# Moving vector-engine work of a two-block transformer kernel from steps with weight sums to steps with whole tiles

## The reference

```python
# block 1
proj = rmsnorm(x, norm_attn) @ w_in            # q, k, v of kinds A and B
ya = dilated_attention(rope(qa), rope(ka), va)
yb = rmsnorm(diff_attention(rope(qb), rope(kb), vb, lam), subln) * (1 - lam_init)
x = x + concat([ya, yb]) @ w_out
x = x + (silu(h @ w_gate) * (h @ w_up)) @ w_down       # h = rmsnorm(x, norm_ffn)
x = rmsnorm(x, norm_final)                             # "norm weighting" of the change
# block 2
proj = rmsnorm(x, attn_norm_w_2) @ w_in_2      # q, k, v, gate of kind R; q, k, v of kind M
o_ret = silu(rg) * normed(retention(rotary(rq), rotary(rk), rv)) * ret_norm_w
x = x + (sigmoid(g_ret) * (o_ret @ w_ret_up) + sigmoid(g_moba) * (o_moba @ w_moba_up)) @ w_out_2
x = x + (silu(a) * b) @ w_ffn_down_2           # a, b: a convolution of h2 @ w_ffn_up_2
```

## Time and profile before

| | |
|---|---|
| median of 3 runs | 2505.69 us (2503.83 to 2507.57) |
| the profiled execution's own time | 2505.64 us |
| its span in the profile | 2503.8 us |
| PE busy | 2477.4 us, 99% |
| PE weight loads busy | 2048.8 us, 82% |
| DVE busy | 2080.5 us, 83% |
| ACT busy | 1498.6 us, 60% |

### The profile page before, as it was taken

One profiled execution on the slowest core, in us unless ns is written; L12 is line 12 of the kernel. 1 busy time (PEld: TensorE's weight loads), 2 busy tenths in 40 slices (PEclk: granted clock), 3 DMA queues, 4 the chain that ended last, 5 costly groups with the idle time before them and its releaser, 6 DMA issues.

```text
span 2503.8 us, 28439 instructions
## 1 busy us (share of the span) xinstructions
PE 2477.4 (99%) x11316; PEld 2048.8 (82%) x11316; DVE 2080.5 (83%) x1701; ACT 1498.6 (60%) x1428; POOL 92.2 (4%) x87
## 2 busy tenths in 40 slices
PE   8999999999999999999999999999999999999998
PEld 7887888888888888887888888888888888888877
DVE  6877567898999998859788757777799999999997
ACT  6544555566666666656465555444565776666665
POOL 0000000000000000010000000000000000000000
PEclk9999999999999999999999999999999999999999
DMA  8446356677777777674545646457565777777773
GB/s 280 164 161 204 132 168 202 197 240 237 237 238 236 239 239 236 221 226 153 201 152 185 235 152 218 164 189 235 169 210 188 217 233 229 233 231 233 231 230 133
DMA packets 259781, 518.28 MB, mean 207 GB/s; under 512 B 8849, under 2 KB 8977, under 8 KB 259393
## 3 DMA queue, kind: packets, MB, share of 16 engines
q1 hardware_dynamic: 238496, 473.05, 55.2%
q0 software_dynamic: 20576, 42.36, 9.2%
q10 hardware_dynamic: 576, 1.05, 0.1%
HBM read 476.57 MB, written 2.10 MB: 191 GB/s over the span
## 4 chain that ended last, share of the span: by engine, by line
PE 89%; DVE 5%; issue 2%; ACT 2%; DMA 1%; SPq 0%; DVEq 0%; ACTq 0%
PE acc L814 21%; PE acc L818 21%; PE acc L816 21%; PE misc L814 5%; PE misc L818 5%; PE misc L816 5%; DVE w_lo L1852 2%; PE misc L859 1%; PE acc L831 1%; PE acc L827 1%; PE acc L829 1%; DMA w_raw<-in_w_in 1%; ACT w_hi L1328 1%; PE misc L867 1%; DVE w_raw L1832 1%
## 5 line engine op out<-in xcount | busy, mean ns | idle before, releaser
L1852 DVE TENSOR_TENSOR w_lo<-w_raw,w_hi 128x2048 fp32r<-128x2048 f32 (+1 forms) x466 | 1045.4, 2253 | 178.5 <-ACT w_hi L1328 177.1
L1328 ACT ACTIVATE w_hi<-w_raw 128x2048 fp32r<-128x2048 f32 (+1 forms) x466 | 879.9, 1891 | 367.4 <-PE acc L818 239.8
L814 PE MATMUL acc<-w_hi,xt_hi 128*128 128x512 f32 x1172 | 464.5, 396 | 6.5 <-ACT qk_stage L1331 2.3
L818 PE MATMUL acc<-w_hi,xt_lo 128*128 128x512 f32 x1172 | 457.8, 391 | 0.0
L816 PE MATMUL acc<-w_lo,xt_hi 128*128 128x512 f32 x1172 | 457.0, 390 | 0.0
L814 PEld LDWEIGHTS acc<-w_hi,xt_hi 128*128 128x128 f32 x1172 | 220.3, 188 | 54.3 <-issue 3.7
L818 PEld LDWEIGHTS acc<-w_hi,xt_lo 128*128 128x128 f32 x1172 | 220.3, 188 | 46.6
L816 PEld LDWEIGHTS acc<-w_lo,xt_hi 128*128 128x128 f32 x1172 | 220.6, 188 | 44.1
L1852 DVE TENSOR_TENSOR w_lo<-w_raw_more,w_hi 128x2048 fp32r<-128x2048 f32 (+1 forms) x101 | 227.1, 2252 | 30.5 <-ACT w_hi L1328 30.4
L1328 ACT ACTIVATE w_hi<-w_raw_more 128x2048 fp32r<-128x2048 f32 (+1 forms) x101 | 191.0, 1892 | 51.7 <-PE acc L818 18.0
L814 PE MATMUL misc<-w_hi,xt_hi 128*128 128x512 f32 x472 | 186.3, 395 | 2.2 <-DVE w_lo L1852 2.2
(11 more groups left out here) (372 smaller groups left out, 4047.5 us busy)
## 6 DMA issues: line engine op xcount, KB each, us to landing
w_raw<-in_w_in SPq DMA_DIRECT2D x136, 1024.0 KB, 5.1
w_raw<-in_w_ffn_up SPq DMA_DIRECT2D x61, 1024.0 KB, 6.3
x<-staged POOLq DMA_DIRECT2D x72, 512.0 KB, 6.2
w_raw<-in_w_gate SPq DMA_DIRECT2D x33, 1024.0 KB, 6.4
w_raw<-in_w_down SPq DMA_DIRECT2D x33, 1024.0 KB, 5.5
w_raw<-in_w_ffn_down SPq DMA_DIRECT2D x33, 1024.0 KB, 5.8
w_raw<-in_w_out SPq DMA_DIRECT2D x32, 1024.0 KB, 5.2
w_raw<-in_w_up SPq DMA_DIRECT2D x27, 1024.0 KB, 5.2
```

The source lines that it names most:

```text
L814: nc.tensor.matmul(bank, hi[:, j, :], w_hi[:, t % RING, j, :], start=first and j == 0, stop=False, skip_group_check=shared)
L818: end = nc.tensor.matmul(bank, lo[:, j, :], w_hi[:, t % RING, j, :], start=False, stop=last and j == C - 1, skip_group_check=shared)
L1328: nc.scalar.activation(w_hi[:, t % RING, rows], raw_tile(steps[t].slot)[:, rows], ACT.Copy).then_inc(hi_ready, 1)
L1852: nc.vector.tensor_tensor(w_lo[:, t % RING, rows], raw_tile(steps[t].slot)[:, rows], w_hi[:, t % RING, rows].bitcast(F32), ALU.subtract).t ...
```

## The change

Nothing is computed differently; pieces are done in other steps.

- Parts 4, 5 and 6 of round 1's attention go from G2, P3 and U3 of round 2 to its v0, v1 and v2.
- All six parts of round 4's attention go to the first six steps of round 5 (q0 to k1). Before they were in U3, G3 and P4 of round 4 and q0, q1 and q2 of round 5.
- The roping of round 4's keys goes from k3 to P2 of round 4, and their transpose on PE from U2 to P4. The roping of round 5's queries goes from q3 to k1, since its scratch `ret_o` is in use until then; their transpose stays at k2.
- Multiplying x by the norm's weights (`gain_quarter`, L1966): before, three quarters in q0 ahead of `xt_lo` and the variance and one behind; now two quarters in q0 behind them and two in q1.
- `s_sums` (L1927 to L1934) goes from q1 to k0 of round 4, `s_hi_piece` from k0 to k2, `s_lo_piece` from k1 to k3.
- In the last step of the first feed-forward part, DVE adds the result to x before it splits the tile.

```diff
@@ -158,8 +158,16 @@
     if r in UNIT_ROUNDS:
-        return ROUND_T[r] + 6, STEP[("round", r), "U2"]
+        return ROUND_T[r] + 6, STEP[("round", r), "P4" if r == 4 else "U2"]
     return ROUND_T[r] + 6, ROUND_T[r] + 9
+
+def rope_step(r, j):
+
+    if r in UNIT_ROUNDS and KIND[r] != "R":
+        return STEP[("round", r), ("U3" if r in P3_ROUNDS else "P7", "P4")[j]]
+    if (r, j) == (4, 1):
+        return STEP[("round", r), "P2"]
+    return ROUND_T[r] + (5 if (r, j) == (5, 0) else 4 * j + 3)
@@ -172,16 +180,13 @@
-             1: [DOWN_T[0] + k for k in range(4)] + early(2, 3),
+             1: [DOWN_T[0] + k for k in range(4)] + [STEP[("round", 2), f"v{k}"] for k in range(3)],
...
-    for r in (4, 5):
-        if r in UNIT_ROUNDS:
-            steps[r] = [STEP[("round", r), name] for name in ("U3", "G3", "P4")] + early(r + 1, 3)
-        else:
-            steps[r] = [ROUND_T[r] + 12 + k for k in range(4)] + early(r + 1, 2)
+    steps[4] = [ROUND_T[5] + k for k in range(6)]
+    steps[5] = [STEP[("round", 5), name] for name in ("U3", "G3", "P4")] + early(6, 3)
@@ -1656,7 +1661,7 @@
-            if t == ROUND_T[4] + 4:
+            if t == ROUND_T[4] + 6:
                 s_hi_piece("rounds2", sa_hi, sa_sum)
@@ -2154,11 +2159,7 @@
-                    if ("round", r) in UNITS and KIND[r] != "R":
-                        roped = STEP[("round", r), ("U3" if r in P3_ROUNDS else "P7", "P4")[j]]
-                    else:
-                        roped = ROUND_T[r] + 4 * j + 3
-                    if t == roped:
+                    if t == rope_step(r, j):
                         rope(r, j)
@@ -2296,9 +2297,12 @@
         for k in range(4):
             t = FFN1_DOWN_T + k
-            split(t + LEAD)
+            if k < 3:
+                split(t + LEAD)
             dve.wait_ge(staged_added[k % 2], 16 * (2 * (NF - 2) + k // 2 + 1))
             add_group(t, ("ffn1_down", NF - 1, k))
+            if k == 3:
+                split(t + LEAD)
@@ -2309,11 +2313,13 @@
-                for q in range(3):
-                    gain_quarter(q)
                 xt_lo_piece(2, 3)
                 variance(2)
                 inverse(2)
+                gain_quarter(0)
+                gain_quarter(1)
+            if t == ROUND_T[4] + 1:
+                gain_quarter(2)
                 gain_quarter(3)
@@ -2324,9 +2330,9 @@
-            if t == ROUND_T[4] + 1:
+            if t == ROUND_T[4] + 4:
                 s_sums("rounds2", 2, a_sum_early, sa_sum)
-            if t == ROUND_T[4] + 5:
+            if t == ROUND_T[4] + 7:
                 s_lo_piece("rounds2", sa_lo, sa_hi, sa_sum)
```

## The result

The changed kernel takes 2509.87 us (median of 15 runs, 2506.24 to 2512.45), the kernel before 2506.01 us on the same chip (15 runs, 2503.83 to 2507.57). The ratio is 1.0019, with a 95% interval of 1.0013 to 1.0026: 3.9 us slower. The prediction said 2508.9 us.

What follows compares the result with a forecast made beforehand. PE's in-line matmuls were taken to bound the kernel, so only PE's waits could move. From 2505.64 us, +0.4 (round 2), −0.3 (rounds 4 and 5) and +3.2 (clock) gave 2508.9 us, range 2504.5 to 2512.5.

Steps and rivals of the forecast that it cites:

- Round 2 without the clock: Round 2: attention paid outside the wait, 3.47 us, less P7 starting 3.07 us earlier; +0.4 us.
- What that load is: Round 2: the load starting at 205.99 and taking 6.91 us was taken for P7's second tile.
- P7 hangs on the load: Round 2: P7 starts only after load, weight sum, split and addition, so its wait grows from 0.66 to 4.8 us.
- Removed waits: Round 4: PE's waits at q1, q3, k1 and two at U2 go, P7's 1.17 us stays; −4.6 us.
- The transposes behind P4: Round 4: the keys' transposes on PE wait for the roping, 8.8 us of chain against 5.44 of matmuls; +3.4 us.
- The queries of round 5: Transpose at k2 of round 5 waits for the roping, 6.35 us against one step's 5.44; +0.9 us.
- The clock: Behind the 4.8 and 3.4 us waits matmuls run at the lower clock, 1.6 us each; +3.2 us.
- The likelier drop behind transposes: Behind P4 of round 4: transposes don't count as work for the clock monitor, so a drop is likelier; no separate size.
- The 5.0 us that I took for what a measurement can tell: Whole kernel: 0.2% of the time, about what a measurement can tell from no change.
- The rival "faster": Behind P4 of round 4: keys roped early, 3.4 us wait and 1.6 us clock unpaid; 2503.9 us, chance 0.05.
- The rival "slower": P7 of round 2 and q0 of round 5: 16 slow matmuls behind each wait, 3.2 us each; 2512.1 us, chance 0.19.

Runs made afterwards that it cites:

- e1: Kernel before with only parts 4, 5 and 6 of round 1's attention moved to v0, v1 and v2 of round 2; 2507.77 us, +2.3 to before.
- e2: Changed kernel with round 1's attention put back into G2, P3 and U3 of round 2; 2507.85 us, +2.4 to before.
- e7: Changed kernel with the weight sum issued in step P7 of round 2 cut to 512 of its 2048 columns; 2507.00 us, +1.0 to before.
- e11: Changed kernel with DVE's addition ahead of the weight sum and split in step P6 of round 2; 2505.32 us, −0.7 to before.
- e6: Kernel before with only the small moves: norm-weighting quarters, activation sums, order of the last split; 2501.47 us, −4.6 to before.
- e3: Changed kernel with 14 idle matmuls on PE ahead of each long wait (round 2's P7, transposes behind round 4's P4); 2505.66 us, +0.2 to before.
- e5: Changed kernel with parts 4, 5 and 6 of round 1's attention in P3, P6 and U3 of round 2; 2503.15 us, −2.9 to before.
- e4: Changed kernel with round 4's keys roped in U3 instead of P2 and transposed after G3 instead of P4; 2505.16 us, −0.3 to before.
- e10: e8 with round 4's keys roped in k3 and transposed after U2, as in the kernel before; 2500.84 us, −4.6 to before.
- e12: e8 with the addition ahead of weight sum and split in every step P6 and in the merges; 2493.61 us, −12.4 to before.
- e8: Changed kernel with the moves of e4 and e5, and round 5's queries transposed after k3 instead of k2; 2497.58 us, −8.5 to before.
- e9: e6 with round 1's attention in P3, P6 and U3 of round 2 as in e5; 2498.91 us, −6.5 to before.

## Why the prediction was right, and where it wasn't

The forecast of 2508.9 us missed the median by 1.0 us, and the waits and the clock stood where it put them. By its terms, each against the profiled execution:

- **Round 2 without the clock**, predicted +0.4. P7 started at 214.38 against 218.13, 3.75 us earlier and not 3.07; with the 3.47 us of attention outside, −0.3. The term was mis-sized by the load: I kept its 6.91 us from the earlier trace rows. In the changed kernel it took 6.27, in e1 5.79 and in e2 5.71.
- **What that load is**, wrong. "The `w_lo` that frees the slot for P7's second tile" should have read P4's tile. P7's weight sum ran at 196.16. The addition merely stands behind P4's weight sum in DVE's queue. The sum didn't suffer, as the order of instructions was read rightly, but "P7 hangs on the load" named a need where there was only a queue: e7 showed whose sum it is, and e11 that P7 starts without the load.
- **Removed waits**, predicted −4.6. All five are gone; P7's of round 4 read 1.6 us against 1.17, so −4.2. e6 shows that the small moves bring nearly all of it (−4.6 by its median).
- **The transposes behind P4**, predicted 3.4. Measured 3.41 us as the view reads it, and so 3.67 by my own way of counting. DVE's chain took the steps foreseen; `w_lo` at 1193.78 to the roping's last instruction at 1199.23 is in the trace as in the sum.
- **The queries of round 5**, predicted 0.9. Measured 0.89 as read, 1.15 counted.
- **The clock**, predicted 3.2 for two drops. Against e3's trace it is 1.6 us at each place, 3.2. e3 gave 3.6 us back when PE was kept busy. The likelier drop behind transposes isn't shown: behind all five waits of 3.4 us ahead of transposes the clock fell (changed kernel, e2, e5, e7, e11), but so it did behind all four waits of 2.57 to 4.06 us at round 2's P7, where none stand (changed kernel, e1, e4, e7).
- **Not in the sum**: the wait for `sig_ret` in merge 2, 0.9 us longer in this execution. e1 to e4 show it between 0.3 and 1.0 us, so it looks like chance; what sets it isn't shown.

Together −0.3 − 4.2 + 3.67 + 1.15 + 3.2 + 0.9 = 4.4, against 4.3 us between the spans. That the forecast came within 1.0 us is in part luck: round 2 gave 0.7 us less than its term, the other waits 0.9 more together, and `sig_ret` 0.9 that no term had. The 5.0 us that I took for what a measurement can tell were too much: the interval of 15 runs is clear of 1 at 3.9 us.

The rival "faster" did not happen, as DVE was not early; e4, which moves the roping, shows what it would have been worth, 4.1 us of its 5.0. The rival "slower", with 16 slow matmuls behind each wait, was not seen in this trace, but it was in part behind the same wait in e5's and e11's. This is e5, first by windows, then PE's timeline:

```profile
1196.20:1197.00 0.80, 0.00 (x0) 0.00 (x0) 0.80 (x2) 0.00 (x0) 0.00 (x0) 0.50 0.96 374
1197.03 1.97 PE L864 MATMUL misc<-ident,qk_stage 128*128 128x128 f32 x8 [3.41 <-DVE qk_stage L2016]
```

Here the clock fell while PE still waited. The transposes take 1.97 us instead of 1.09, and the nine products behind them are slow. From the first transpose to the eleventh product is 5.97 us in e5 and 6.04 in e11, against 3.23 in e3 and 4.81 in the changed kernel. So a wait of 3.4 us cost 2.7 and 2.8 us by the clock there, and 1.6 here.

## What to carry to other kernels

An engine that is busy 99% of the time can still hide work: whatever stands in front of a wait that something else sets is free, and moving it behind the wait only makes the wait longer (e10, and the change itself in round 2). Before calling a wait a dependency, look at what stands ahead of the awaited instruction in its own queue; here an addition of 0.75 us, ready to run, stood behind another tile's load, and putting it first took P7's waits away in every round that had one (e12). And if the matmul engine must wait long, something harmless to do is cheaper than rest, since the clock that it loses is paid afterwards (e3).

## What the runs showed of the hardware

The length of a wait alone does not decide whether the clock falls. Ahead of low-clock stretches PE had been idle for 1.76 us (e11), 1.87 (e4), 1.94 (e5), 2.28 (e6), 2.29 (before), 2.56 (e10), 3.41 and 3.87 us (changed kernel); but behind a wait of 2.30 us in e2, at the same place as those of before and e6, it did not fall, nor behind those of 1.65 and 1.68 us in the changed kernel and e2, at the place of e4's, e5's and e11's. PE's timeline of e2:

```profile
199.56 0.50 PE L819 MATMUL acc<-w_hi,xt_hi 128*128 128x512 f32 x1 [2.30 <-ACT qk_stage L1336]
199.90 0.40 PE L821 MATMUL acc<-w_lo,xt_hi 128*128 128x512 f32 x1
200.14 0.40 PE L823 MATMUL acc<-w_hi,xt_lo 128*128 128x512 f32 x1
```

All next matmuls keep 0.23 us. This agrees with the sentence of the Trainium skill, page "TensorE: Matmul & The Clock Gate", section "What's actually happening", that the monitor runs free of the kernel.

It may also show in the spread, but the runs don't settle it. The changed kernel's runs lie between 2506.24 and 2512.45 us, 6.2 apart. Its four runs with a mean granted clock of 0.996 or 0.997 took 2511.83 to 2512.45 us, the eleven with 0.998 took 2506.24 to 2511.87. e8's and e12's traces hold no low clock until PE's last matmul is done, and their runs lie between 2497.31 and 2498.29, and 2493.28 and 2494.02 (5 runs each), under 1 us apart. But e3's and e9's traces hold none either, and their runs lie 3.2 (11 runs) and 2.6 us (7 runs) apart. So the clock seems to have a part in the changed kernel's spread, and how much of the rest it makes is not shown.
